# Recurrent stage of a hybrid decoder layer: one filler unit moved from the last head's end to the running sums, and a second accumulator bank for the first five units

## Chip, cores and metric

One Trainium2 chip, one NeuronCore. The metric is the device time of one execution in microseconds (us). Engine names in the rows: PE is TensorE (PEld its weight loads), DVE is VectorE, ACT is ScalarE, POOL is GpSimd, SP is SyncE.

## What is computed

One inference step of one decoder layer: 512 prompt tokens and 8 x 4 sample tokens (544 in all), model width 1024. The change touches the stage that computes the mLSTM branch. Cut to what matters here:

```python
# recurrent branch, per head h of 4 (DQK = 128, DV = 256)
b     = cumsum(log_f)                        # running sums over the tokens
m_t   = max(b + m, max_s(b_t - b_s + i_s))   # running maximum
s     = (q @ k.T) * exp(d_log - m_t)
num   = w_inter * (q @ C) + s @ v
C_new = a * C + (w * k).T @ v                # new state, also an output
y_a   = norm(num / max(|den|, exp(-m_t))) * norm_a_g * sigmoid(a_o)
# merge gates, needed two stages later
gates = sigmoid(x @ w_merge)                 # (544, 1024) @ (1024, 2048)
# next stage: learned block compressor of raw key/value pages
kc, vc = einsum(pages + pe, w_cmp)
```

## The kernel before

The program is a row of stages; between two stages all engines meet at a barrier. `stage_project` makes q, k, v and the gates' inputs, `stage_mlstm` (295 to 474 us of the profile) the recurrent branch, `stage_compress` (to 498 us) the block compressor, then attention, merging, a layer norm and the expert layer follow, which takes most of the time.

In `stage_mlstm` TensorE has two kinds of work. The recurrent products of the four heads depend on VectorE and ScalarE at many places. The **filler** is `x @ w_merge`, which depends on nothing of the stage: 16 weight tiles of 128 columns, each for two token halves of 256 and 288, make 32 **units**, numbered u = 0 to 31 (tile n = u // 2). A unit is 8 steps of 3 matmuls (high and low parts of both operands), 24 matmuls into one accumulator of PSUM. `fill(key)` issues the steps that the table `fill_at` gives to a place in the program: "scan" (before the running sums are used), "cols" (behind the small products that turn the sums into columns), and for each head the places "c", "e3" to "e0", "g", "u" and "end". Evens have 256 tokens, odds 288.

Around each unit other engines work in their own fixed order:

- ScalarE copies the finished accumulator to the staging tile `gate_stage` (`gates`, L1034; semaphore `g_evac`), and behind every odd unit of tile n it makes the high part of tile n + 2 (`high`, L1024).
- GpSimd makes the low part of that tile (`low`, L678); tile n's low part overwrites its raw weights.
- SyncE stores `gate_stage` (L652) once the odd unit's copy is made, and loads the weights of tile n + 3 (L641). All its transfers are issued in one fixed order. After the store of tile 15 come three loads for the next stage: `bqT` (L664, 2176 KB) and the two halves of the compressor's weights `wc` (L666, 1024 KB each), then four key/value pages `xs` (L671, 256 KB each), which wait until head 3's new state has been written out.

VectorE's part ahead of head 0 is a chain on four partitions: two ScalarE functions of the forget gate, two `tensor_tensor_scan` (L892, L894), then short operations up to `abr` (L906), which sets `m_ready`. TensorE waits for `m_ready` at L780, makes some 20 small products of 1 to 32 columns (L780 to L789), and goes on with the "cols" unit and head 0 (L798). Every head after that follows the same pattern; its last recurrent products are two groups at L847 that update the sample states, with the unit "u" between them and the unit "end" behind them. After head 3 TensorE turns two small results (L856, L857) and waits for the normalised rows (L870), which depend on a VectorE chain (L953 to L994), a square root on ScalarE (L1069) and 15 ScalarE scalings (L1075).

In `stage_compress` SyncE (L1137) and ScalarE (L1276) issue the last eight pages of 256 KB at the stage's start; TensorE's first series of 128 matmuls (`cmpX`, L1189) waits for `wc`, the second (`xs`, L1189) for all 16 pages.

Of the kernel before, what the change touches and what calls it, by code (L numbers as in the profile page):

```python
# [33 lines left out]
AH, DQK, DV = 4, 128, 256  # L34
# [505 lines left out]
def stage_mlstm(nc, s, io):  # L540
# [48 lines left out]
    gst = at("gate_stage", 8704, [P, 2, T])  # L589
    GT = 2 * DC  # L590
    fill_at, filled = {}, 0
    for key, steps in ([("scan", 24), ("cols", 8)] +
                       [((h, k), n) for h in range(AH)
                        for k, n in (("c", 16), ("e3", 8), ("e2", 4), ("e1", 4), ("e0", 4), ("g", 4), ("u", 8), ("end", 8))]):
        fill_at[key] = (filled, filled + steps)
        filled += steps
    assert filled == 16 * GT
# [2 lines left out]
    with ExitStack() as ctx:  # L600
# [18 lines left out]
        gwh_done, gwl_done, g_psum, g_evac, bq_in = (sem("gw_high"), sem("gw_low"), sem("gate_psum"), sem("gate_evac"),  # L619
                                                     sem("bq_in"))  # L620
        g_sent = [sem("g_sent0"), sem("g_sent1")]
        ps = ctx.enter_context(nc.psum_tensor("ps_m", [P, 8, 512], F32))
        block = ctx.enter_context(nc.Block())

        score_at = [(2, 0), (3, 0), (4, 0), (4, 256)]
        update_bank = [0, 5, 2, 3]

        def done_tiles(key):

            return range(fill_at[key][0] // 16, fill_at[key][1] // 16)  # L630
# [116 lines left out]
        def _(pe):  # L747
            def fill(key):

                for step in range(*fill_at[key]):  # L750
                    u, dc = step // 8, step % 8
                    n, half = u // 2, u % 2
                    t0, nt = TSPLIT[half]
                    out, toks = ps[:, 1, 0:nt], slice(t0, t0 + nt)
                    if dc == 0:
                        if n >= 2:
                            pe.wait_ge(gwl_done, n - 1)
                        if u:
                            pe.wait_ge(g_evac, u)
                    pe.matmul(out, gw_hi[:, n % 2, dc, :], s.xTh[:, dc, toks], start=(dc == 0), stop=False)  # L760
                    pe.matmul(out, gw_hi[:, n % 2, dc, :], s.xTl[:, dc, toks], start=False, stop=False)
                    last = pe.matmul(out, gw_lo[:, n % 3, dc, :], s.xTh[:, dc, toks], start=False, stop=(dc == DC - 1))
                    if dc == DC - 1:
                        last.then_inc(g_psum, 1)

            def slot(k):

                if k >= 2:
                    h, x = (k - 2) // 6, (k - 2) % 6
                    if 1 <= x <= 4:  # L770
                        pe.wait_ge(out_act, 4 * h + x)
                    else:
                        pe.wait_ge(out_dve, 2 * h + 1 + x // 5)
                return ps[:, 6 + k % 2, :]
# [18 lines left out]
            for h in range(AH):  # L793
# [24 lines left out]
                out = slot(6 * h)  # L818
# [6 lines left out]
                for k, j in enumerate((3, 2, 1, 0)):  # L825
# [3 lines left out]
                    out = slot(6 * h + 1 + k)  # L829
# [5 lines left out]
                out = slot(6 * h + 5)  # L835
# [185 lines left out]
        def _(act):  # L1021
# [4 lines left out]
            def gates(key):  # L1026

                for u in range(fill_at[key][0] // 8, fill_at[key][1] // 8):
                    n, half = u // 2, u % 2
                    t0, nt = TSPLIT[half]  # L1030
                    act.wait_ge(g_psum, u + 1)
                    if half == 0 and n >= 2:
                        act.wait_ge(g_sent[n % 2], 16 * (n // 2))
                    act.copy(gst[:, n % 2, t0:t0 + nt], ps[:, 1, 0:nt]).then_inc(g_evac, 1)  # L1034
                    if half == 1 and n + 2 < GT:
                        high(n + 2)

# [2247 lines left out]
```

## Time and profile before

| | us |
|---|---|
| median of 3 runs | 2167.01 (2165.47 to 2167.32) |
| profiled execution, its own time | 2169.9 |
| span of the profiled execution, first to last instruction | 2168.2 |
| mean granted TensorE clock in it | 0.988 of full speed |

Times in the rows are counted from the span's start. A row of a timeline that ends in [x <-E] says that the engine sat idle for x us before it and that an operation of engine E ended the wait. PEclk is the granted TensorE clock: 1.00 stands for 2.4 GHz, 0.50 for 1.2 GHz.

### The profile page before, as it was taken

What the parts mean: (1) busy time and instruction counts of PE and PEld (TensorE: products, weight loads), DVE (VectorE), ACT (ScalarE), POOL (GpSimd) and SP (SyncE); (2) the same over time, 40 slices, a digit from 0 to 9 for tenths busy, and PEclk for the clock granted to TensorE, in tenths of its full rate; (3) what the DMA queues carried; (4) which work ended last, traced back from release to release, by engine and by line L of the source; (5) the groups of instructions that cost most, each with busy time, mean ns of one, the idle gap of its engine ahead of it and who ended that gap; (6) DMA issues with size and microseconds to landing.
All of it is one profiled execution on the core that took longest, in us unless ns stands there. A gap on an engine that the chain in (4) does not pass through costs nothing.

```text
span 2168.2 us, 34384 instructions
## 1 busy us (share of the span) xinstructions
PE 2093.0 (97%) x13308; PEld 1861.3 (86%) x13308; DVE 1482.0 (68%) x3070; ACT 986.9 (46%) x1763; POOL 916.7 (42%) x615
## 2 busy tenths in 40 slices
PE   9999999978998998999999999999999999999998
PEld 8898988865655986999999999999998887888886
DVE  4334242456777455498889979876648899888886
ACT  2122322225777231333346666676544554445542
POOL 1000222331110001346877677777765555555530
PEclk9999999988999999999999999999999999999999
DMA  4354333456010533326889899999999999999992
GB/s 146 95 197 117 104 117 119 140 206 156 2 41 22 204 112 130 106 75 234 298 266 313 297 347 312 330 382 402 370 331 389 404 405 379 394 399 396 388 364 80
DMA packets 191242, 518.58 MB, mean 239 GB/s; under 512 B 15796, under 2 KB 85544, under 8 KB 186600
## 3 DMA queue, kind: packets, MB, share of 16 engines
q1 hardware_dynamic: 139656, 330.80, 43.4%
q0 software_dynamic: 50848, 184.53, 22.8%
q8 instruction: 106, 1.74, 0.3%
q10 hardware_dynamic: 576, 1.05, 0.1%
q14 instruction: 56, 0.46, 0.1%
HBM read 446.70 MB, written 73.75 MB: 240 GB/s over the span
## 4 chain that ended last, share of the span: by engine, by line
PE 56%; DVE 3%; ACT 0%; POOL 0%; issue 0%; DVEq 0%
PE ps_e L2559 24%; PE ps_e L2534 8%; PE ps_e L2529 7%; PE ps_e L2528 7%; PE ps_e L2551 3%; PE ps_e L2583 1%; PE ps_e L2589 1%; PE ps_e L2594 1%; PE ps_e L2590 1%; PE ps_e L2517 1%; DVE row L2924 1%; DVE one_b L2908 0%; DVE one_a L2908 0%; POOL u_lo L2477 0%; DVE oh L2842 0%
## 5 line engine op out<-in xcount | busy, mean ns | idle before, releaser
L2470 POOL DMA_INDIRECT row<-in_peer_v,sparse_idx x160 | 273.6, 1710 | 210.9 <-DVE y L2932 159.5
L2528 PE MATMUL ps_e<-hTh,u_hi 128*128 128x384 f32 x1024 | 347.1, 339 | 0.0
L2529 PE MATMUL ps_e<-hTl,u_hi 128*128 128x384 f32 x1024 | 346.7, 339 | 0.0
L2477 POOL TENSOR_TENSOR u_lo<-u_raw,u_hi 128x1024 fp32r<-128x1024 f32 x128 | 313.9, 2454 | 65.6 <-ACT u_hi L2634 56.9
L2559 PE MATMUL ps_e<-v_hi,w_hi 128*128 128x512 f32 x768 | 242.4, 397 | 0.0
L2559 PE MATMUL ps_e<-v_lo,w_hi 128*128 128x512 f32 x768 | 240.7, 394 | 0.0
L2559 PE MATMUL ps_e<-v_hi,w_lo 128*128 128x512 f32 x768 | 240.6, 394 | 0.0
L2952 DVE TENSOR_TENSOR v_lo<-v_raw,v_hi 128x1024 fp32r<-128x1024 f32 x128 | 158.1, 1237 | 85.0 <-ACT v_hi L2673 84.6
L2534 PE MATMUL ps_e<-hTh,u_lo 128*128 128x384 f32 x1024 | 207.7, 345 | 3.8 <-POOL u_lo L2477 3.8
L2673 ACT CAST v_hi<-v_raw 128x1024 fp32r<-128x1024 f32 x128 | 128.2, 1048 | 154.7 <-DMA v_raw<-in_peer_v 154.7
L2924 DVE CUSTOM_DVE_ANT_0 row<-row,ps_e 128x1024 f32<-128x1024 f32 x150 | 178.6, 1214 | 24.6 <-DMA row<-in_peer_u,sparse_idx 22.8
L2470 POOL DMA_INDIRECT row<-in_peer_u,sparse_idx x150 | 153.5, 1024 | 98.4 <-DVE sparse_hid L2924 75.7
L2528 PEld LDWEIGHTS ps_e<-hTh,u_hi 128*128 128x128 f32 x1024 | 193.0, 189 | 0.0
L2529 PEld LDWEIGHTS ps_e<-hTl,u_hi 128*128 128x128 f32 x1024 | 193.0, 189 | 0.0
L2534 PEld LDWEIGHTS ps_e<-hTh,u_lo 128*128 128x128 f32 x1024 | 176.4, 188 | 4.5 <-POOL u_lo L2477 4.5
L2559 PEld LDWEIGHTS ps_e<-v_hi,w_hi 128*128 128x128 f32 x768 | 145.1, 189 | 34.3 <-issue 0.8
L2559 PEld LDWEIGHTS ps_e<-v_lo,w_hi 128*128 128x128 f32 x768 | 144.6, 188 | 34.7
L2559 PEld LDWEIGHTS ps_e<-v_hi,w_lo 128*128 128x128 f32 x768 | 144.5, 188 | 33.8
L2932 DVE SCALAR_TENSOR_TENSOR y<-row,sparse_w,y 128x1024 f32<-128x1024 f32 x128 | 164.3, 1283 | 8.6 <-DMA row<-in_peer_v,sparse_idx 5.1
L250 PE MATMUL ps_proj<-xT_hi,w_hi 128*128 128x256 f32 (+2 forms) x528 | 151.8, 287 | 2.2 <-DVE xT_lo L332 1.7
L251 PE MATMUL ps_proj<-xT_lo,w_hi 128*128 128x256 f32 (+2 forms) x528 | 152.3, 289 | 0.0
L252 PE MATMUL ps_proj<-xT_hi,w_lo 128*128 128x256 f32 (+2 forms) x528 | 152.0, 288 | 0.0
(557 smaller groups left out, 4536.0 us busy)
## 6 DMA issues: line engine op xcount, KB each, us to landing
u_raw<-in_peer_uT SPq DMA_DIRECT2D x128, 512.0 KB
v_raw<-in_peer_v SPq DMA_DIRECT2D x30, 2048.0 KB, 10.4
hidden_gelu<-gelu_out SPq DMA_DIRECT2D x64, 384.0 KB
gate_tables<-g_buf SPq DMA_DIRECT2D x48, 512.0 KB
e_gate<-gate_tables SPq DMA_DIRECT2D x31, 768.0 KB
gelu_in<-hidden_gelu SPq DMA_DIRECT2D x31, 768.0 KB
w_raw<-in_w_tiles SPq DMA_DIRECT2D x45, 512.0 KB, 3.6
gw_raw<-in_merge_tiles SPq DMA_DIRECT2D x16, 512.0 KB, 3.9
```

Source lines behind the costliest of these rows:

```text
L250: pe.matmul(out, hi, s.xTh[:, dc, toks], start=(dc == 0), stop=False)
L251: pe.matmul(out, hi, s.xTl[:, dc, toks], start=False, stop=False)
L252: last = pe.matmul(out, lo, s.xTh[:, dc, toks], start=False, stop=(dc == DC - 1))
L2470: pool.indirect_dma_start(out=row[:, :], out_offset=None, in_=io.peer_u if i < U_END else io.peer_v, in_offset=bass.IndirectOffsetOnAxis(a ...
L2477: pool.tensor_tensor(u_lo[n % UB][:, :, :], u_raw[n % UB][:, :, :], u_hi[:, n % UH, :, :].bitcast(F32), ALU.subtract).then_inc(ul_done, 1)
L2528: pe.matmul(ps[:, n % 2, 0:TD], u_hi[:, n % UH, dc, :], hTh[:, dc, :], start=(dc == 0), stop=False)
L2529: pe.matmul(ps[:, n % 2, 0:TD], u_hi[:, n % UH, dc, :], hTl[:, dc, :], start=False, stop=False)
L2534: last = pe.matmul(ps[:, n % 2, 0:TD], u_lo[n % UB][:, dc, :], hTh[:, dc, :], start=False, stop=(dc == DC - 1))
L2559: last = pe.matmul(ps[:, 2 * t + half, :], w[u][:, c, ts], v[u][:, c, half * 512:(half + 1) * 512], start=(g == 0 and c == 0 and w is whi ...
L2924: dve.tensor_tensor_reduce(out=row, in0=row, in1=ps[:, 4:6, :], scale=1.0, scalar=0.0, op0=ALU.mult, op1=ALU.add, accum_out=hid[:, c:c + 1 ...
L2932: dve.scalar_tensor_tensor(out=acc, in0=row, scalar=wsp[:, c:c + 1], in1=acc, op0=ALU.mult, op1=ALU.add)\
L2952: dve.tensor_tensor(v_lo[g % 2][:, c, :], v_raw[g % 2][:, c, :], v_hi[g % 2][:, c, :].bitcast(F32), ALU.subtract).then_inc(vl_done, 1)
```

## The change

Three edits. The table gives the "scan" place 32 steps instead of 24 (units 0 to 3 instead of 0 to 2) and head 3's "end" none instead of 8; every place between thus works on the unit with the next number. The units 0, 2 and 4 accumulate in PSUM bank 7, all others in bank 1 as before. The wait ahead of a unit follows: unit 1 waits for no copy any more, units 2 to 5 for the copy of the unit before the last, later ones for the last as before.

```diff
-    for key, steps in ([("scan", 24), ("cols", 8)] +
+    for key, steps in ([("scan", 32), ("cols", 8)] +
                        [((h, k), n) for h in range(AH)
-                        for k, n in (("c", 16), ("e3", 8), ("e2", 4), ("e1", 4), ("e0", 4), ("g", 4), ("u", 8), ("end", 8))]):
+                        for k, n in (("c", 16), ("e3", 8), ("e2", 4), ("e1", 4), ("e0", 4), ("g", 4), ("u", 8),
+                                     ("end", 8 if h < AH - 1 else 0))]):
...
+        def fill_bank(u):
+
+            return 7 if u in (0, 2, 4) else 1
...
-                    out, toks = ps[:, 1, 0:nt], slice(t0, t0 + nt)
+                    out, toks = ps[:, fill_bank(u), 0:nt], slice(t0, t0 + nt)
                     if dc == 0:
                         if n >= 2:
                             pe.wait_ge(gwl_done, n - 1)
-                        if u:
+                        if u >= 6:
                             pe.wait_ge(g_evac, u)
+                        elif u >= 2:
+                            pe.wait_ge(g_evac, u - 1)
...
-                    act.copy(gst[:, n % 2, t0:t0 + nt], ps[:, 1, 0:nt]).then_inc(g_evac, 1)
+                    act.copy(gst[:, n % 2, t0:t0 + nt], ps[:, fill_bank(u), 0:nt]).then_inc(g_evac, 1)
```

**ScalarE, from the forget gate's logarithm (L1041) to the columns' exponentials (L1045).** The names in brackets are the semaphores waited for; a hardware semaphore used again shows the name of its first use, so x_in1, x_in7 and gw_in0 to gw_in2 are only labels. Before:

```order
L1041 ACTIVATE lfrow<-lfrow 4x544 [waits x_in1]
L1034 COPY gate_stage<-ps_m 128x256 [waits gate_psum]
L1034 COPY gate_stage<-ps_m 128x288 [waits gate_psum]
L1024 CAST gw_hi<-gw_raw 128x1024 [waits gw_in2]
L1034 COPY gate_stage<-ps_m 128x256 [waits gate_psum]
L1045 ACT_TABLE_LOAD
L1045 ACTIVATE en<-ps_m 128x16 [waits x_in7]
```

And in the changed program, whose lines are numbered 7 higher here:

```order
L1048 ACTIVATE lfrow<-lfrow 4x544 [waits x_in1]
L1041 COPY gate_stage<-ps_m 128x256 [waits gate_psum]
L1041 COPY gate_stage<-ps_m 128x288 [waits gate_psum]
L1031 CAST gw_hi<-gw_raw 128x1024 [waits gw_in2]
L1041 COPY gate_stage<-ps_m 128x256 [waits gate_psum]
L1041 COPY gate_stage<-ps_m 128x288 [waits gate_psum]
L1031 CAST gw_hi<-gw_raw 128x1024 [waits gw_in0]
L1052 ACT_TABLE_LOAD
L1052 ACTIVATE en<-ps_m 128x16 [waits x_in7]
```

The copy of unit 3 and the high part of tile 3, with its wait for that tile's load, now stand ahead of the columns' exponentials; before they stood behind them.

**GpSimd, from the marks of the sample states to the first operands of the state products.** Before:

```order
L710 TENSOR_TENSOR inside<-inside 128x2 [waits sample_marks]
L678 TENSOR_TENSOR gw_lo<-gw_raw,gw_hi 128x1024 [waits gw_high,sample_marks]
L715 DMA out_p_m<-brow 4x1 [waits x_in6]
L716 DMA out_s_m<-brow 4x8x1
L685 TENSOR_SCALAR kws<-kn,wsi 128x128
```

After:

```order
L715 TENSOR_TENSOR inside<-inside 128x2 [waits sample_marks]
L683 TENSOR_TENSOR gw_lo<-gw_raw,gw_hi 128x1024 [waits gw_high,sample_marks]
L683 TENSOR_TENSOR gw_lo<-gw_raw,gw_hi 128x1024 [waits gw_high]
L720 DMA out_p_m<-brow 4x1 [waits x_in6]
L721 DMA out_s_m<-brow 4x8x1
L690 TENSOR_SCALAR kws<-kn,wsi 128x128
```

The low part of tile 3 moved ahead of the two small stores and of the first head's operands.

**TensorE, from head 3's last full unit to the turned results.** Before:

```order
L762 MATMUL ps_m<-xT_hi,gw_lo 128x256
L847 MATMUL ps_m<-vn,kwb 128x257 [waits stage_out0]
L847 MATMUL ps_m<-vn,kwb 128x257 x3
L760 MATMUL ps_m<-xT_hi,gw_hi 128x288 [waits gate_evac,gw_low]
L761 MATMUL ps_m<-xT_lo,gw_hi 128x288
...
L856 MATMUL ps_m<-ident,nout 32x128 [waits stage_out0,proj_psum,stage_out1]
L857 MATMUL ps_m<-ident,pn 4x128
```

After:

```order
L769 MATMUL ps_m<-xT_hi,gw_lo 128x288
L854 MATMUL ps_m<-vn,kwb 128x257 [waits stage_out0]
L854 MATMUL ps_m<-vn,kwb 128x257 x3
L863 MATMUL ps_m<-ident,nout 32x128 [waits stage_out0,proj_psum,stage_out1]
L864 MATMUL ps_m<-ident,pn 4x128
```

The 24 matmuls of the "end" unit are gone from this place; unit 31 is now the one ahead of the second update group. SyncE's order is the same in both programs: only the events that it waits for come at other times.

## Rows read from the trace of the kernel before

**Rows 1.** Timeline of TensorE, running sums: start, length, engine, line, operation, [idle before it]

```profile
295.37 0.35 PE L760 MATMUL ps_m<-xT_hi,gw_hi 128*128 128x256 f32 x1 [2.10 <-PEq L78]
...
299.55 0.40 PE L760 MATMUL ps_m<-xT_hi,gw_hi 128*128 128x288 f32 x1 [1.10 <-ACT gate_stage L1034]
...
303.51 0.39 PE L760 MATMUL ps_m<-xT_hi,gw_hi 128*128 128x256 f32 x1 [0.49 <-ACT gate_stage L1034]
...
307.62 0.22 PE L780 MATMUL ps_m<-ident,brow 4*128 4x4 f32 x1 [0.99 <-DVE abr L906]
```

**Rows 2.** Timelines of ScalarE, GpSimd and VectorE, one after another, same stretch

```profile
303.35 1.05 ACT L1024 CAST gw_hi<-gw_raw 128x1024 fp32r<-128x1024 f32 x1
...
304.55 2.43 POOL L678 TENSOR_TENSOR gw_lo<-gw_raw,gw_hi 128x1024 fp32r<-128x1024 f32 x1 [6.46 <-ACT gw_hi L1024]
...
302.17 1.28 DVE L894 TENSOR_TENSOR_SCAN mrow<-lift_mask,arow 4x544 f32<-4x544 f32 x1
...
304.65 2.35 DVE L904 COPY rows<-mrow 4x32 f32<-4x32 f32 x1
...
307.41 0.15 DVE L906 TENSOR_TENSOR abr<-m,mrow 4x8 f32<-4x8 f32 x1
```

**Rows 3.** Sums over stretches: length, each engine's busy us, then PEclk, DMA share, GB/s

```profile
307.00:312.00 5.00, 4.38 (x30) 4.32 (x31) 0.67 (x8) 1.32 (x2) 0.00 (x0) 0.66 0.15 61
312.00:318.00 6.00, 6.00 (x29) 5.04 (x29) 0.41 (x4) 1.68 (x8) 2.64 (x5) 0.72 0.02 3
298.00:304.00 6.00, 4.41 (x32) 3.97 (x32) 4.47 (x6) 2.43 (x5) 0.09 (x1) 1.00 1.02 335
```

**Rows 4.** Timeline of TensorE at the end of head 3

```profile
456.57 0.50 PE L847 MATMUL ps_m<-vn,kwb 32*128 32x257 f32 x4
...
460.39 0.29 PE L762 MATMUL ps_m<-xT_hi,gw_lo 128*128 128x288 f32 x1
```

**Rows 5.** Timelines of VectorE, then ScalarE, behind head 3

```profile
461.67 0.24 DVE L989 TENSOR_SCALAR rstd<-den 128x16 f32<-128x16 f32 x2
...
461.14 1.28 ACT L1069 ACT_TABLE_LOAD   x1
...
463.64 0.60 ACT L1075 ACTIVATE hn<-vn,nbias,rstd 128x256 f32<-128x256 f32 x1 [0.90 <-DVE nbias L994]
```

**Rows 6.** Timeline of SyncE's DMA queue (SPq), end of this stage, start of the next

```profile
461.14 0.33 SPq L652 DMA_DIRECT2D gate_pre<-gate_stage  x1
461.52 1.26 SPq L664 DMA_DIRECT2D bqT<-bq_rows  x1
462.82 1.71 SPq L666 DMA_DIRECT2D wc<-in_w_cmp  x2
...
474.91 3.65 SPq L1137 DMA_DIRECT2D xs<-in_cache_cmp_T  x4
```

**Rows 7.** Sums over stretches around those transfers, columns as in rows 3

```profile
457.00:461.00 4.00, 3.90 (x34) 3.35 (x26) 3.46 (x15) 0.33 (x2) 0.93 (x1) 1.00 0.00 0
461.00:476.00 15.00, 6.10 (x40) 5.60 (x40) 10.91 (x34) 9.20 (x19) 2.79 (x24) 0.88 1.00 385
476.00:484.00 8.00, 6.18 (x128) 6.10 (x128) 7.36 (x26) 0.00 (x0) 7.58 (x12) 0.58 1.02 380
484.00:486.00 2.00, 0.41 (x8) 0.41 (x10) 1.43 (x8) 0.00 (x0) 0.57 (x1) 1.00 0.06 20
```

**Rows 8.** The view of tile xs, 440 to 500 us: issue to landing

```profile
DMA to landing us min/median/max: 2.9/6.0/11.5
```

**Rows 9.** Timeline of TensorE in the compression stage, and where attention begins

```profile
477.64 6.18 PE L1189 MATMUL ps_c<-cmpX,wc 128*64 128x33 f32 x128 [5.76 <-DMA wc<-in_w_cmp]
485.59 8.87 PE L1189 MATMUL ps_c<-xs,wc 128*64 128x128 f32 x128 [1.78 <-DMA xs<-in_cache_cmp_T]
...
498.58 0.49 PE L1414 MATMUL ps_a<-kslT,bqT 64*128 64x128 f32 x4 [1.86 <-PEq L78]
```

**Rows 10.** Sums over a stretch of TensorE's second series there

```profile
486.00:490.00 4.00, 4.00 (x48) 4.00 (x46) 0.00 (x0) 0.00 (x0) 0.00 (x0) 0.57 0.00 0
```

## Prediction

> **What bounds the kernel now.** I read the sums by stretch first, for the two places that the change touches, then the timeline of each engine there, and then followed the consequence through the transfers into the next stage. Most of the time is TensorE's work in the expert layer, which the change doesn't touch; what is won or lost between 295 and 498 us is carried through the stage barriers as it is. Three places count.
>
> *Running sums.* TensorE has nothing of its own until `m_ready` and works on units 0 to 2. It stops three times: 1.10 us ahead of unit 1 and 0.49 us ahead of unit 2, each time until ScalarE has emptied the one accumulator bank, and 0.99 us until VectorE has finished `abr` [rows 1]. VectorE is no faster because of GpSimd: the copy at 304.65 us takes 2.35 us for 32 columns and ends at 307.00, when GpSimd's low part ends (304.55 + 2.43 = 306.98) [rows 2].
>
> *Small products.* From 307.62 us on TensorE makes products of few columns, and the granted clock falls: a mean of 0.66 over 5 us and 0.72 over the next 6 us [rows 3]. At the low level, 1.2 GHz or 0.50, that is (1 - 0.66) / 0.5 x 5 = 3.4 us and (1 - 0.72) / 0.5 x 6 = 3.4 us, 6.8 us at half speed, or 3.4 us of lost work.
>
> *The last head.* The last unit's last matmul starts at 460.39 us [rows 4], but nobody on the recurrent path waits for it: VectorE's chain goes on to 461.67 + 0.24 = 461.91 us, and the scalings on ScalarE start at 463.64 us [rows 5]. What does wait for it is SyncE. The store of the last gate tile is issued at 461.14 us, and queued right behind it, in the fixed order, are `bqT` and `wc` [rows 6]. In the four microseconds before that the DMA engines carry nothing; then they are full, at 385 and 380 GB/s, until 484 us [rows 7]. That backlog is what TensorE waits for in the next stage: 5.76 us for `wc`, 1.78 us for the pages [rows 9].
>
> **Part by part.** *Two banks and a fourth unit in the running sums.* Units 1 and 2 take, to their modelled ends, 303.51 - 0.49 - 299.55 = 3.47 us and 307.62 - 0.99 - 303.51 = 3.12 us [rows 1]. Back to back each loses its tail and its restart, about 0.25 us together by the spacing of the matmuls, so a pair costs 6.1 us. Units 0 to 3 then run without a stop (unit 2 needs unit 0's copy, unit 3 needs unit 1's, both long made) from 295.37 to 307.6 us: the stops of 2.6 us and the tails pay for a whole unit.
>
> Is `m_ready` in time? Unit 1 ends about 1.4 us earlier, so the high part, at 303.35 us now, starts at 302.0, and the low part on GpSimd at 303.2 instead of 304.55 us. VectorE is then in the scan of 302.17 + 1.28 = 303.45 us [rows 2]. The rest of the chain stands behind GpSimd until 303.2 + 2.43 = 305.6 us, and needs the 1.9 us that it needs now without the stop (from 303.45 to 307.41 + 0.15 = 307.56, less 2.2): ready at 307.5. If GpSimd also has to wait for the scan, it ends at 303.45 + 2.43 = 305.9 and `m_ready` comes at 307.8. The small products start between 307.6 and 307.9 instead of 307.62 us: 0 to +0.3, I take +0.1, since a step of 0.3 needs a wait that no row shows. The Trainium skill ("SBUF — State Buffer", Who interferes with whom) says that the pair of ports that VectorE and GpSimd share is held for a whole instruction, also by a VectorE operation with two inputs in SBUF, and that the later one waits. By that rule GpSimd would wait for the scan, and the step would be the 0.3; it speaks against the change, but for little.
>
> *The copy of unit 3 and tile 3's high part on ScalarE* (1.5 us) now stand ahead of the columns' exponentials, and its low part ahead of `prepare` on GpSimd. TensorE's "cols" unit covers them: they end near 309.2 us, the columns' results come at 310 us or later, and `cols_read` is wanted only behind the unit, at 313 us. If tile 3's load is late this cover is gone (third rival).
>
> *Clock.* The idle time ahead of the small products goes; they themselves stay, some 2.5 us at full speed. Bounds: the fall stays as it is, 0, or the clock stays up, -3.4 us [rows 3]. The fall is not made by idle time alone: TensorE was busy for 4.38 of the 5 us [rows 3], and it falls again behind a pause of only 1.78 us and matmuls of 33 columns (0.57 of full clock over 486 to 490 us) [rows 9, 10]. So I expect the small products to bring it down in most executions, sometimes for one period instead of two: -0.8 us. The Trainium skill ("TensorE: Matmul & The Clock Gate", The HAM clock gate) calls the low level the idle one and has the clock follow how busy TensorE has been. Read as "busy is busy", the changed stretch, without idle time, would keep 2.4 GHz and the whole 3.4 us come back; the row of 4.38 busy us at 0.66 speaks against that reading.
>
> *The heads.* Between the small products and head 3's second update group lie 14 units of each size, before and after, so nothing changes there but the parity: each tile's high and low part fall one unit earlier in the program. Heads 0 and 2 take the pattern of 1 and 3, and the other way round. 0 us.
>
> *The missing "end" unit.* TensorE saves 4 us where it was not awaited: 0. ScalarE no longer copies unit 31 late, so its table load (461.14 + 1.28 = 462.42 us) is over before VectorE is ready at 461.91 us [rows 5]: the root, the scalings and the stage's end come 0.5 us earlier, with the +0.1 above 0.4.
>
> *Transfers.* Unit 31 now ends where unit 30 ended, just before 456.57 us [rows 4], 3.9 us (4.0 less the 0.1) ahead of now. With it go the store, `bqT` and `wc`, issued from 457.2 us on, into the empty DMA time. From 461 to 486 us pass 15 x 385 + 8 x 380 + 2 x 20 = 8.85 MB [rows 7]; eight pages of 256 KB, 2.1 MB, are those issued at the next stage's start. Of the other 6.75 MB some 1.35 MB (3.8 us at 350 GB/s) have gone before 461 us, so they are done at 461 + 5.4 / 0.385 = 475.0 us. `wc` lands about 3.5 us earlier, near 474 us, when the stage begins: the first series starts at once and is over before the pages are in. The pages are issued from 474.91 - 0.4 = 474.5 us on [rows 6]. A page alone takes 2.9 us to land [rows 8], 0.7 of it data, so new data flow from 476.7 us at the latest and last 2.1 / 0.38 = 5.5 us: 482.2 us instead of 484.2, -2.0 with a gap, and -3.5 if only the last issue counts (now at 474.91 + 3.65 - 0.34 = 478.2, then at 477.8, + 2.9 = 480.7 us). I take -2.6, nearer the first, since the bytes bind more than the issues. This contains the 0.4 us above, not adding to it. The second series starts near 483.0 instead of 485.59 us.
>
> **Sum.** -2.6 (pages) - 0.8 (clock) = -3.4 us, and attention begins at 495.2 instead of 498.58 us [rows 9]. The profiled execution took 2169.9 us, so 2166.5 in its terms; the runs' median is 2.9 us lower, which gives 2163.6 us.
>
> **Rivals.** 1. *The clock stays up* through the small products. For it: no idle time is left around them. Against: rows 3 and 10. Worth -2.6 - 3.4 = -6.0: 2161.0 us. Chance 0.18.
> 2. *The early transfers buy next to nothing.* The second series needs all pages, and the last are tied to the stage's start; if the pages still take their median 6.0 us [rows 8] from the issue, only the 0.4 us arrive, with the clock's 0.8 a gain of 1.2: 2165.8 us. For it: they still queue behind each other. Against: that median was measured behind a backlog that is now gone. Chance 0.20.
> 3. *Slower: tile 3's load is late.* It is issued some 2 us earlier than now, near 302.6 us, behind two state loads that keep the DMA engines full (1.02 from 298 to 304 us) [rows 3], and ScalarE now waits for it ahead of the exponentials. By its bytes it lands near 307 us, wanted at 308.1. It decides once it lands after some 311 us, for then `cols_read` misses 313 us; each microsecond beyond costs one, and from 315 us on the gain is gone. At 317 us: 2169 us. Chance 0.05.
> 4. *The forecast*: 0.57, with its own range of 2161.8 to 2165.6, which takes in the pages' bounds and one clock period more or less (1.7 us) in the second series, where the pause ahead may grow from 1.78 to 3 us.
>
> **Numbers.** 0.2% of 2167 is 4.3 us, about what a measurement of this kernel can tell from no change. Faster by more than that: rival 1 and a quarter of the forecast's case, 0.33. Slower by more: 0.04. Within it: 0.63. The range that leaves two in ten out reaches from rival 1's upper half to rival 2: 2160.2 to 2166.6 us.
>
> **What would show it.** In the changed kernel's profile: no stop of TensorE between 295.4 and 307.6 us; GpSimd's low part at 303.2 to 303.5 and a VectorE operation of over 2 us behind it; the clock over 307 to 318 us (0.66 and 0.72 now); the store, `bqT` and `wc` near 457.2 us with transfers from there on; TensorE's first series at about 474 without a wait for `wc`, its second near 483 us. The forecast is wrong if the second series starts after 485, if head 0 begins later than 316.8 us, or if the later stages don't keep the distance.

## The result, and the profile after

The changed kernel takes 2172.3 us (median of 14 runs, 2167.92 to 2178.08), the kernel before 2168.16 us on the same chips (14 runs, 2165.47 to 2172.84; the three runs shown ahead of the prediction had a median of 2167.01). The ratio is 1.0022, 95% interval 1.0015 to 1.0029: slower by 4 to 5 us, where 3.4 us faster was forecast. The profiled execution took 2173.22 us, with a span of 2171.5 us.

The running sums went as intended. The timeline of TensorE there, then those of VectorE, GpSimd and ScalarE, to be held against [rows 1, 2]:

```profile
295.10 0.55 PE L767 MATMUL ps_m<-xT_hi,gw_hi 128*128 128x256 f32 x1 [2.09 <-PEq L78]
...
299.52 0.29 PE L767 MATMUL ps_m<-xT_hi,gw_hi 128*128 128x288 f32 x1
...
308.83 0.22 PE L787 MATMUL ps_m<-ident,brow 4*128 4x4 f32 x1
...
301.90 1.28 DVE L901 TENSOR_TENSOR_SCAN mrow<-lift_mask,arow 4x544 f32<-4x544 f32 x1
304.48 2.38 DVE L912 TENSOR_TENSOR rows<-m,mrow 4x32 f32<-4x32 f32 x1
307.16 0.16 DVE L913 TENSOR_TENSOR abr<-m,mrow 4x8 f32<-4x8 f32 x1
...
304.40 2.41 POOL L683 TENSOR_TENSOR gw_lo<-gw_raw,gw_hi 128x1024 fp32r<-128x1024 f32 x1 [6.58 <-ACT gw_hi L1031]
...
309.60 1.04 ACT L1031 CAST gw_hi<-gw_raw 128x1024 fp32r<-128x1024 f32 x1 [0.26 <-DMA gw_raw<-in_merge_tiles]
```

No matmul of the four units has an idle time behind it any more, and the small products follow unit 3 at once. Unit 0 alone ran at half clock in this execution, but for its last matmuls (it takes 299.52 - 295.10 = 4.42 us; with full clock it takes 2.93 us, as in experiments 1 and 12), which is why they start at 308.83 and not at 307.6 us. The sums over stretches, with columns as in [rows 3]:

```profile
295.00:298.50 3.50, 3.40 (x16) 3.43 (x17) 1.28 (x2) 3.40 (x4) 2.40 (x9) 0.51 0.09 14
307.00:312.00 5.00, 5.00 (x48) 4.79 (x47) 0.68 (x8) 2.73 (x3) 1.28 (x1) 1.00 0.68 190
312.00:318.00 6.00, 6.00 (x29) 4.83 (x28) 0.69 (x3) 0.93 (x7) 3.67 (x6) 0.72 0.19 71
```

The clock is up over 307 to 312 us (0.66 before), though until 308.83 us that stretch still holds matmuls of unit 3. TensorE is at the low clock for 3.4 us here, where it was for 6.8 us before, and that gives back what unit 0 lost: the second update group of head 3 starts at 456.21 us, where [rows 4] has 456.57. Up to here the change is level or 0.4 us ahead. What follows is the timeline of SyncE's queue, and then GpSimd's issue of head 3's state store, against [rows 6]:

```profile
456.74 0.33 SPq L657 DMA_DIRECT2D gate_pre<-gate_stage  x1
457.11 0.43 SPq L669 DMA_DIRECT2D bqT<-bq_rows  x1
457.59 0.94 SPq L671 DMA_DIRECT2D wc<-in_w_cmp  x2
473.58 3.65 SPq L676 DMA_DIRECT2D xs<-in_cache_cmp_T  x4
479.18 3.65 SPq L1144 DMA_DIRECT2D xs<-in_cache_cmp_T  x4
...
459.16 0.91 POOL L739 DMA_DIRECT2D out_s_C<-c  x1 [19.63 <-DVE nout L964]
```

The kernel before has, for the store and then for GpSimd's first operation in the next stage:

```profile
459.52 0.93 POOL L734 DMA_DIRECT2D out_s_C<-c  x1 [14.20 <-DVE nout L957]
...
474.20 0.20 POOL L1142 TENSOR_SCALAR_AFFINE_SELECT hm<-ones 128x16 f32<-128x16 f32 x1 [8.08 <-POOLq L78]
```

The view of waits over 440 to 500 us has this line for SyncE's queue in the changed kernel (us in total, times, longest):

```profile
SPq L674 <- DMA out_s_C<-c: 14.3, 1, 14.3
```

`bqT` is issued 4.4 us earlier, where 3.9 were forecast. But SyncE then waits 14.3 us for the landing of `out_s_C`, the state store of head 3, because it may load pages 4 to 7 only once that state has been written out (`c_sent[1]`); the kernel before has there:

```profile
SPq L669 <- DMA out_s_C<-c: 0.2, 1, 0.2
```

The store is issued 0.36 us earlier than before and takes 13.7 us to land. Why it does is seen in the DMA queues over windows (packets, MB, share of 16 engines); q1 carries SyncE's transfers, q0 GpSimd's. The changed kernel over 459 to 462, 462 to 465 and 465 to 468 us:

```profile
q1 hardware_dynamic: 58, 1.01, 94.1%
...
q1 hardware_dynamic: 51, 0.89, 84.6%
q0 software_dynamic: 17, 0.07, 5.6%
...
q1 hardware_dynamic: 109, 0.80, 64.4%
q0 software_dynamic: 107, 0.44, 35.4%
```

and the kernel before over the first two of them:

```profile
q0 software_dynamic: 82, 0.34, 30.3%
...
q0 software_dynamic: 190, 0.71, 67.2%
q1 hardware_dynamic: 111, 0.24, 32.8%
```

Before, the store has the DMA engines to itself from 461 to 464 us; the packets of q1 in the second window are those of the gate store (0.24 MB / 111, 2 KB each), and `bqT` comes behind them. Now the engines are full of `bqT` when the store is issued; its first packet comes behind 464 us, some 5 us after the issue (one-microsecond windows show none before), and from there on the two queues get the same number of packets, 107 and 109. A packet of the store is 4 KB (0.44 MB / 107), one of `bqT` 17 KB (0.89 MB / 51), one of `wc` 8 KB (0.27 MB / 33 over 468 to 469 us), so an equal number of packets is a third of the bytes or less for the store.

TensorE in the next stage, then GpSimd's first operation there, against [rows 9]:

```profile
478.65 5.79 PE L1196 MATMUL ps_c<-cmpX,wc 128*64 128x33 f32 x128 [7.59 <-PEq L78]
487.99 9.65 PE L1196 MATMUL ps_c<-xs,wc 128*64 128x128 f32 x128 [3.56 <-DMA xs<-in_cache_cmp_T]
...
501.75 0.49 PE L1421 MATMUL ps_a<-kslT,bqT 64*128 64x128 f32 x4 [1.86 <-PEq L78]
...
478.47 0.20 POOL L1149 TENSOR_SCALAR_AFFINE_SELECT hm<-ones 128x16 f32<-128x16 f32 x1 [13.22 <-POOLq L78]
```

SyncE's four page issues end at 473.58 + 3.65 = 477.2 us, and the stage's barrier opens only then: GpSimd begins at 478.47 us, where the kernel before has 474.20. TensorE waits for the barrier and no longer for `wc`. The last eight pages go out 479.18 - 474.91 = 4.3 us later, the second series starts 2.4 us later, runs 0.8 us longer at a lower clock, and attention begins 501.75 - 498.58 = 3.2 us later. The span is 3.3 us longer: the rest of the kernel adds nothing.

### The profile page after: what moved, and what is told of

Its sections match the earlier page's. It is cut to its first block, busy times and chain, and to the rows that moved or that the text cites. A ratio compares the mean times of both kernels' runs of the same rounds, so it can differ in the third digit from the quotient of the medians.

```text
span 2171.5 us, 34384 instructions
## 1 busy us (share of the span) xinstructions
PE 2093.4 (96%) x13308; PEld 1862.3 (86%) x13308; DVE 1485.0 (68%) x3070; ACT 987.6 (45%) x1763; POOL 920.5 (42%) x615
## 4 chain that ended last, share of the span: by engine, by line
PE 56%; DVE 3%; ACT 0%; POOL 0%; issue 0%; DVEq 0%
PE ps_e L2566 24%; PE ps_e L2541 8%; PE ps_e L2536 7%; PE ps_e L2535 7%; PE ps_e L2558 3%; PE ps_e L2590 1%; PE ps_e L2596 1%; PE ps_e L2601 1%; PE ps_e L2597 1%; PE ps_e L2524 1%; DVE row L2931 1%; DVE one_b L2915 0%; DVE one_a L2915 0%; POOL u_lo L2484 0%; DVE oh L2856 0%
## 6 DMA issues: line engine op xcount, KB each, us to landing
gelu_in<-hidden_gelu SPq DMA_DIRECT2D x31, 768.0 KB, 13.2
```

## The experiments

Theory S, formed from these rows: the moved unit does what it was meant to do, and the loads that it releases early overtake the state store, whose landing holds SyncE, the pages and the barrier. Its rival U: the unit, the second bank or the clock costs the time, and the store is a by-product. Each experiment's time is a median of 5 to 12 runs; the kernel before ran beside them, at 2168.80 (first four experiments), 2168.10 (next four), 2168.95 (next three) and 2168.82 us (last).

**1. The store ahead of the loads**, in the changed kernel, by SyncE instead of GpSimd:

```
+            sp.wait_ge(c_new, AH)
+            sp.dma_start(io.s_C[:, AH - 1]..., c0[:, (AH - 1) % 2, :, 0:DV]).then_inc(c_last, 16)
             sp.dma_start(s.bqT[:, :, :], io.bq_rows).then_inc(bq_in, 16)
...
-            sp.wait_ge(c_sent[1], 32)
+            sp.wait_ge(c_last, 16)
```

> The changed kernel, but head 3's new state is written out by SyncE, ahead of bqT and wc in its own queue, instead of by GpSimd. Theory S (in the changed kernel this store stands behind bqT and wc in the DMA engines, lands at 473 us instead of about 465, and holds up the four pages and the stage's end): the store lands near 464 us, the four pages are issued near 464 to 468 us, the compression stage begins near 473.5 us and its second series near 483 to 484 us; the time is 1 to 3.5 us below the kernel before. Rival U (the moved unit or the bank itself costs the time, in the sums, the heads or the clock): the second series may come earlier, but the time stays 3 to 5 us above the kernel before.

2167.31 us, ratio to the kernel before 0.9996 (0.9988 to 1.0005). The store lands 5.3 us after its issue at 458.99 us, SyncE waits 1.9 us for it, and attention begins at 495.66 us. The 4 us are gone, as S expected, with the moved unit and both banks in place; whether it is faster than the kernel before, which S also expected (by 1 to 3.5 us), this run does not show, since its interval holds 1.

**2. The banks alone**: the last filler unit stays at head 3's end, the banks alternate.

```
-    for key, steps in ([("scan", 32), ("cols", 8)] +
+    for key, steps in ([("scan", 24), ("cols", 8)] +
...
-                                     ("end", 8 if h < AH - 1 else 0))]):
+                                     ("end", 8))]):
```

> The two banks alone; the table of units is that of the kernel before. Theory S: unit 31 and the loads behind it stay where they were, TensorE only waits longer for the running sums (until about 307.6 us), so the time is within 1 us of before. Rival U: running the first units back to back costs 2 us or more by itself, by a later end of the running sums or a lower clock.

2168.09 us, ratio 1.0001 (0.9992 to 1.001), no difference. The gate store goes out at 459.87 us, behind the state store's issue, and SyncE waits 0.2 us for the latter.

**3. The move alone**, made in the kernel before, with its one bank:

```
-    for key, steps in ([("scan", 24), ("cols", 8)] +
+    for key, steps in ([("scan", 32), ("cols", 8)] +
...
-                        for k, n in (..., ("u", 8), ("end", 8))]):
+                        for k, n in (..., ("u", 8), ("end", 8 if h < AH - 1 else 0))]):
```

> The moved unit alone, with one bank. The three stops of the running sums stay, so unit 3 ends near 310.5 us, and everything behind it is 2.5 to 3 us later than in the changed kernel. Theory S: unit 31 still ends ahead of head 3's new state, the store still queues behind bqT and wc (over 10 us to landing), and the time is 6 to 8 us above before. Rival U, if the bank is what costs: the time is nearer to before than the changed kernel's, under +4 us.

2174.2 us, ratio 1.0027 (1.0017 to 1.0038). SyncE waits 13.7 us for the store, the barrier comes at 479.4, attention at 503.80 us. The move alone brings the loss; the direction and the wait are as S expected, the size (5.4 us of medians) is a little under its 6 to 8. About 1 us of it is not the store's: with one bank the four units stop three times, and the second update group of head 3 starts at 457.60 us instead of 456.57.

**4. The kernel before with a late store**: nothing is moved, but GpSimd issues head 3's store only once the last gate tile has landed.

```
                 pool.wait_ge(c_new, h + 1)
+                if h == AH - 1:
+                    pool.wait_ge(g_sent[1], 16 * DC)
```

> The kernel before, but GpSimd holds head 3's state store until the last gate tile has landed, which is when bqT and wc are already queued. No unit is moved. Theory S: the store takes 10 us or more, the four pages are issued at 474 us or later, the compression stage begins at 479 us or later, and the time is 5 us or more above before. Rival U: no unit was moved, so the time is within 1 us of before.

2177.98 us, ratio 1.0042 (1.0029 to 1.0055). GpSimd issues the store at 463.32 us, behind `bqT` and `wc`. SyncE's wait, and then the timeline of TensorE with the next stage's two series:

```profile
SPq L669 <- DMA out_s_C<-c: 15.4, 1, 15.4
```

```profile
483.62 6.84 PE L1191 MATMUL ps_c<-cmpX,wc 128*64 128x33 f32 x128 [12.15 <-PEq L78]
494.37 10.10 PE L1191 MATMUL ps_c<-xs,wc 128*64 128x128 f32 x128 [3.91 <-DMA xs<-in_cache_cmp_T]
```

The same kind of wait, and a barrier 9.2 us later than in the kernel before (GpSimd begins at 483.44 us), with no unit moved: the order of store and loads is enough by itself. The store's later issue, by 3.8 us, would not have been by itself: had it landed after 5.3 us as in experiment 1, the pages would have been issued by some 472.3 us (an estimate, 463.32 + 5.3 + 3.65), ahead of the old barrier at 474.20. Instead the pages go out at 478.56 us.

**5. Small rows**: in the changed kernel `bqT` comes in eight transfers with rows of 2 KB.

```
-            sp.dma_start(s.bqT[:, :, :], io.bq_rows).then_inc(bq_in, 16)
+            for q in range(BH // 2):
+                sp.dma_start(s.bqT[:, q, :], io.bq_rows[:, q, :]).then_inc(bq_in, 16)
...
-            sp.wait_ge(bq_in, 16)
+            sp.wait_ge(bq_in, 16 * (BH // 2))
```

> The changed kernel, with bqT (2176 KB) loaded by eight transfers whose rows are 2176 bytes instead of one whose rows are 17 KB. Theory S (the head-3 state store comes late because its packets of 4 KB take turns, one for one, with packets of 17 KB and 8 KB, and the page loads behind it hold the stage barrier): beside bqT the store now gets some two thirds of the bytes instead of a fifth, and lands 6 to 9 us after its issue instead of 13.7; the last four pages are issued at 466 to 469 instead of 473.6 us, the barrier no longer waits for SyncE, and the kernel gives back most of the loss: 0 to 1.5 us above the kernel before. Rival Q (what counts is only how many bytes were handed to the engines ahead of the store, not the size of their packets): the eight issues still come before 460.5 us, the store still takes over 11 us, pages at 471 us or later, and the kernel stays 3 to 5 us above the kernel before.

2169.68 us, ratio 1.0006 (0.9997 to 1.0015). The store lands 9.8 us after its issue instead of 13.7, the pages go out at 468.68 us, the barrier no longer waits for SyncE, attention begins at 494.66 us. The queues of this kernel over 464 to 467 us:

```profile
q0 software_dynamic: 207, 0.82, 66.5%
q1 hardware_dynamic: 214, 0.43, 36.8%
```

Again an equal number of packets, but now they are two thirds of the bytes for the store. Rival Q, bytes ahead and nothing else, falls by these counts, not by the landing time: 9.8 us lies between S's 6 to 9 and Q's 11 or more, and eight issues take SyncE so long that `wc` goes out at 459.99 us, behind the store's issue at 458.13, so there were also fewer bytes ahead. The first packet of the store still comes some 4 us or more after its issue (one packet in the window from 462 us, 49 in the next). The median, 1.6 us above the kernel before, doesn't show the attention's early start: the profiled execution took 2165.57 us, but seven of the eleven runs took 2169.6 us or more, and why is open.

**6. The kernel before with SyncE's store** (the edit of experiment 1).

> The kernel before, with head 3's state store issued by SyncE ahead of bqT, as in the run of the changed kernel with that edit. It tells what the moved unit is worth once the store comes first. Theory S: in the kernel before the store came first anyway, so only little changes, within 1.5 us of the kernel before; the last gate tile still ends at 461.1 us, bqT is issued near 461.9 us, the attention begins at 497.5 to 499 us, some 2 to 3 us later in the profile than in the changed kernel with the same edit (495.66). Rival W (the gain of that run came from the store's queue and not from the earlier transfers): the attention begins here at 496.5 us or earlier, and the time is the same as that of the changed kernel with the edit.

2169.77 us, ratio 1.0009 (1.0 to 1.0018), 1.7 us above the kernel before and so just outside S's 1.5; `bqT` issued at 461.77 us, attention at 499.22 us. SyncE can issue the store only behind the last gate store, at 461.30 us, 1.8 us later than GpSimd did. Rival W falls: the gain of experiment 1 isn't the store's queue.

**7. The changed kernel with SyncE's store again**, on the same chip as 6.

> The changed kernel with SyncE's store ahead of bqT, once more, on the chip of the other three, to be set against the kernel before with the same edit. Theory S with the forecast's gain left over: attention begins at 495.5 to 496.5 us, and the time is 0 to 3 us under the kernel before and 1 to 3 us under the kernel before with this edit. Rival: the 2.9 us at the attention's start are not carried to the end, and both kernels with SyncE's store take the same time within 1 us.

2167.08 us, ratio 0.9994 (0.9985 to 1.0003), attention at 494.93 us. With SyncE's store in both kernels, the whole change (moved unit and banks) is worth 2169.77 - 2167.08 = 2.7 us of medians: all eleven runs here took under 2168.3 us, ten of the eleven of experiment 6 over 2168.5. Attention comes 4.3 us earlier in the profiled executions, 1.3 us of it because the second series ran at full clock here (7.21 us) and not there (8.54). Part of the 2.7 us is what SyncE's late store costs experiment 6: against the unchanged kernel before, this one is 1.0 us faster, within the interval. And what the moved unit adds to the banks no run shows: on one chip, experiments 1 and 2 differ by 0.8 us, far less than their runs scatter.

**8. The loads level with the store**: one more wait in the changed kernel, on the state.

```
+            sp.wait_ge(c_new, AH)
             sp.dma_start(s.bqT[:, :, :], io.bq_rows).then_inc(bq_in, 16)
```

> The changed kernel with one more wait: SyncE issues bqT and wc only once head 3's new state is ready (459.0 us by the run with SyncE's store), 2.2 us later than in the changed kernel and about with the store on GpSimd's queue. Nothing else moves. Theory S gives a dose between: the store has a head start or an even start, lands 6 to 11 us after its issue (13.7 in the changed kernel), the last four pages are issued at 466 to 471 us, and the time is -1 to -4 us against the changed kernel. Rival U (the moved unit itself, or the clock at the stage's start, costs the 4 us): the same time as the changed kernel or later, 2172 us or more.

2174.03 us, ratio 1.003 (1.0018 to 1.0041): by its time alone, what U expected. This expectation of S was wrong, and the trace shows why. SyncE and GpSimd issue:

```profile
457.22 0.32 SPq L670 DMA_DIRECT2D bqT<-bq_rows  x1
...
457.49 0.91 POOL L740 DMA_DIRECT2D out_s_C<-c  x1 [19.63 <-DVE nout L965]
```

Over 460 to 462 us, and then over 463 to 464 us, the engines carry this:

```profile
q1 hardware_dynamic: 46, 0.80, 96.2%
...
q1 hardware_dynamic: 16, 0.28, 75.1%
q0 software_dynamic: 18, 0.07, 17.8%
```

Not one packet of the store in 4.5 us, then one for one with `bqT`, a fifth of the bytes, and it lands after 14.6 us. An issue at the same moment is no even start: GpSimd's store needs 1.5 us or more to its first packet on free engines, and three times that on full ones. So the head start had to be larger, and the two theories were still to be parted by it. One part of U falls here: unit 0 ran at full clock (1.00 over 295 to 298.5 us), and the time was lost all the same.

**9. The loads 2.4 us behind the store**: the same wait, on VectorE's sums under the roots.

```
+            sp.wait_ge(var_ready, 2)
             sp.dma_start(s.bqT[:, :, :], io.bq_rows).then_inc(bq_in, 16)
```

> The changed kernel, with SyncE holding bqT and wc until VectorE has the sums under the square roots ready (some 461.4 us, 2.3 us behind the state store's issue; in the kernel before the distance is 2.0 us). The run that held them only until the state was ready kept them level with the store, and the store's first packet still came 5 us after its issue. Theory S (the transfers' order at the engines): with the head start of before, the store's first packets come within 2 us of its issue and it lands 5 to 7 us after it, the pages are issued near 465.5 us, SyncE no longer holds the barrier, and the time is within 1.5 us of the kernel before, 3 to 5 us below the changed kernel. Rival U (the moved unit, the second bank or the clock costs the 4 us): the same time as the changed kernel, 3 us or more above the kernel before.

2166.6 us, ratio 0.9994 (0.9985 to 1.0003). SyncE, GpSimd's issue, then TensorE:

```profile
459.42 0.32 SPq L670 DMA_DIRECT2D bqT<-bq_rows  x1
459.79 1.69 SPq L672 DMA_DIRECT2D wc<-in_w_cmp  x2
463.10 3.65 SPq L677 DMA_DIRECT2D xs<-in_cache_cmp_T  x4
471.60 3.65 SPq L1145 DMA_DIRECT2D xs<-in_cache_cmp_T  x4
...
457.04 0.91 POOL L740 DMA_DIRECT2D out_s_C<-c  x1 [19.63 <-DVE nout L965]
...
474.78 6.20 PE L1197 MATMUL ps_c<-cmpX,wc 128*64 128x33 f32 x128 [5.90 <-DMA wc<-in_w_cmp]
482.69 8.87 PE L1197 MATMUL ps_c<-xs,wc 128*64 128x128 f32 x128 [1.71 <-DMA xs<-in_cache_cmp_T]
...
495.67 0.49 PE L1422 MATMUL ps_a<-kslT,bqT 64*128 64x128 f32 x4 [1.86 <-PEq L78]
```

and its queue over 459 to 461 us:

```profile
q0 software_dynamic: 171, 0.70, 98.0%
```

The store lands in 5.3 us, and with all parts of the change in place the kernel is 5.6 us faster than the changed kernel (2172.18 us, below). A wait added, and nothing else: rival U is out. Another rival for the late first packet, that VectorE's work holds up GpSimd's store, falls too: VectorE is busy for 3.26 of the 4 us from 457 us here and for 3.28 in experiment 8, in the same chain of operations, and only here do packets come within 2 us of the issue.

**10. The loads behind the store's landing**: the wait is on `c_sent[1]`, and SyncE issues `bqT` at 466.03 us.

> The changed kernel, with SyncE holding bqT and wc until the state store has landed, near 464.8 us. The other end of the dose: the store is undisturbed, the pages are issued right behind, and nothing of the forecast's early transfers is left: bqT and wc come 3.3 us later than in the kernel before. Theory S: the store lands 5 to 6 us after its issue, wc some 2 to 3 us later than in the kernel before, the second series starts near 487 to 488 us, and the time is 1 to 3 us above the kernel before, still below the changed kernel by 1 to 3 us. Rival U: as its 4 us stay and the late loads come on top, 6 us or more above the kernel before.

2169.48 us, ratio 1.0001 (0.9992 to 1.001). The store lands in 5.0 us, `wc` is waited for 7.40 us, the second series starts at 488.22 and attention at 499.54 us. As late as that the loads cost what the change gains, and the kernel is still 2.7 us under the changed one. Against the kernel before it is 0.5 us slower, where S expected 1 to 3.

**11. The changed kernel once more**, beside 9 and 10.

> The changed kernel once more, beside the two kernels with held loads and on their chip: 3.5 to 5.5 us above the kernel before, store landing 13 to 15 us after its issue, attention beginning near 501.5 us. Both theories expect the same of it; it is the level against which the other two are read.

2172.18 us, ratio 1.0017 (1.0008 to 1.0026), 3.2 us above the kernel before, a little less than expected; the store takes 13.2 us, attention begins at 501.72 us.

**12. Experiment 9 once more**, on another chip.

> The changed kernel with bqT and wc held until the sums under the square roots are ready, once more, to see whether it is under the kernel before or only level with it. Theory S with the forecast's gain left over: 1 to 3.5 us under the kernel before (2.35 us of medians in the first run), attention beginning between 495.5 and 498 us. Rival: the first run's distance was its chip's, and this one is level with the kernel before within 0.7 us.

2166.69 us, ratio 0.9995 (0.9985 to 1.0004), attention at 494.20 us, earlier than the 495.5 expected. Both times the median is some 2 us under that of the kernel before (2.35 and 2.13), and both intervals hold 1: that this version is faster than the kernel before is likely, not shown; that it is faster than the changed kernel is shown.

**The traces from a common start.** The profiled executions reach unit 0 at different times, from 294.79 to 296.97 us, so up to 2.2 us between two of the times above is made ahead of this stage. Here they are counted from the start of unit 0; the barrier is GpSimd's first operation of the next stage. The last column is the median less that of the kernel before beside it.

| kernel | unit 0 starts | barrier | second series | attention | median |
|---|---|---|---|---|---|
| before | 295.37 | 178.8 | 190.2 | 203.2 | |
| changed | 295.10 | 183.4 | 192.9 | 206.7 | +4.1 |
| changed once more (11) | 294.93 | 182.9 | 193.0 | 206.8 | +3.2 |
| move alone (3) | 295.18 | 184.0 | 194.9 | 208.6 | +5.4 |
| before, late store (4) | 295.12 | 188.3 | 199.3 | 213.5 | +9.2 |
| loads level (8) | 294.92 | 182.8 | 193.7 | 207.9 | +5.9 |
| before, SyncE's store (6) | 295.15 | 179.3 | 191.4 | 204.1 | +1.7 |
| loads behind the landing (10) | 296.97 | 179.3 | 191.3 | 202.6 | +0.5 |
| small rows (5) | 295.56 | 178.3 | 187.8 | 199.1 | +1.6 |
| banks alone (2) | 296.48 | 177.3 | 188.2 | 199.5 | -0.7 |
| SyncE's store (1) | 296.70 | 176.4 | 187.6 | 199.0 | -1.5 |
| SyncE's store again (7) | 296.24 | 176.4 | 187.4 | 198.7 | -1.0 |
| loads 2.4 us behind (9) | 296.00 | 174.9 | 186.7 | 199.7 | -2.4 |
| the same again (12) | 294.79 | 176.5 | 188.1 | 199.4 | -2.1 |

The five rows in which the store goes out level with the loads or behind them, with their large packets, have the barrier at 182.8 us or later, and all others at 179.3 or earlier: theory S holds on this count as well. But the traces set the better kernels some 4 us ahead of the kernel before, where the medians say 1 to 2.4, or nothing for the banks alone. In part this is the clock of one execution: the second series took 7.21 us in experiments 1, 2, 5, 7, 10 and 12, and 8.54 to 8.87 us in experiments 6 and 9 and in the kernel before.

## Why the prediction was wrong, and where it was right

*Running sums* (units back to back, small products +0.1): right. There is no stop, and the four units take 13.7 us instead of the forecast's 12.2, of which 1.5 is unit 0 at half clock. In experiments 1, 5, 7, 8, 9 and 12, with unit 0 at full clock, they take 12.2 us. The half clock doesn't need the change: the kernel of experiment 4, with nothing moved, has 0.57 over 295 to 298.5 us, and that of experiment 9, with all of it, 1.00. But both traces of the changed kernel itself have 0.51, so that it is chance is not shown. GpSimd's low part was to be at 303.2 to 303.5 us; it came at 304.40, by unit 0's delay, and the operation of VectorE that started right behind it took 2.38 us for 32 columns, as in [rows 2]. The Trainium skill ("SBUF — State Buffer", Who interferes with whom) has it that of two operations that need the shared ports the later one waits for the whole of the first. The trace agrees here, with GpSimd's operation ending at 306.81 and VectorE's at 306.86 us. The other collision that it was cited for, with the scan, could not be seen: the scan was over at 303.2 us.

*Tile 3's high part*: covered, as forecast. Its load held ScalarE for 0.26 us only; the slower rival named there played no part.

*Clock*: under-sized. Forecast were 0.8 us; over 307 to 312 us the granted clock went from 0.66 to 1.00, (1.00 - 0.66) x 5 = 1.7 us at 2.4 GHz, and over 312 to 318 us it stayed at 0.72. Weighed over the 11 us, nine of the ten executions with 32 steps have 0.85, the banks alone 0.84, and the three with neither 0.69, so half of the low stretch goes nearly always, not sometimes. The tenth, that of experiment 9, has 1.00: there the forecast's first rival came true. Stops ahead of the small products don't decide this by themselves, as the move alone has three of them (1.10, 0.49 and 0.46 us) and 0.85 too. The gain didn't reach the end in the changed kernel, as unit 0 used it up.

*The heads* and *the missing unit* at head 3's end: right. The second update group moved by -0.36 us and the scalings on ScalarE from 463.64 to 462.78 us.

*Transfers* (-2.6 us): this step failed. It said that the store of the last gate tile, `bqT` and `wc` go "into the empty DMA time", and worked out from bytes alone when they are through, and it took the stage's end and the pages' issue at 474.5 us as free of them. The time was empty because the state store of head 3 had not been issued yet; it is issued at 459.5 us, in the middle of the 3.9 us by which the loads were to come forward, and SyncE's next instruction waits for it. The step counted what moves with the gate store and passed over what it moves past: the store's 1 MB is in its 6.75 MB, but with no place in the order and nobody who waits for it. In place of 474.5 us the pages went out at 479.18 us, +4.3 instead of -0.4, and the 2.6 us of gain became 2.4 us of loss, with 0.8 us more from the lower clock of the second series. That series began at 487.99 us, past the 485 us that the forecast had named as the sign of being wrong. The rival that ended on the slower side named another load in another place; this mechanism was not among the cases.

Where the order is kept, the forecast's total nearly comes out: in experiments 1, 7, 9 and 12 attention begins 3.5 to 4.5 us earlier than before, counted from unit 0, where it has 3.4, and the medians give 1.0 to 2.4. That the traces come near is in part luck, since the parts are others. In experiments 1, 7 and 12 the second update group comes 1.6 us earlier (159.6 us from unit 0 instead of 161.2), which is the clock, twice its 0.8. The second series starts 2.1 to 2.9 us earlier, so the transfers add 0.5 to 1.3 us, not 2.6. The rest, 8.87 - 7.21 = 1.7 us, is the clock of the second series, which the forecast had in its range only. The sum of bytes is not tested by this: with the order safe no run had the loads go out more than some 3.4 us earlier (experiments 1 and 7), and what the full head start would be worth stays open.

That packets decide how the two queues share, and not bytes, could have been read beforehand. The Trainium skill ("DMA: Bandwidth & Descriptors", Queues, rings and completion order) says that a DMA engine takes turns between the queues that have work for it, one packet each. The trace agrees, with 107 packets against 109 here, 207 against 214 in experiment 5 and 18 against 16 in experiment 8. With the packet sizes of the traces this makes a third of the bytes for the store beside `wc` and a fifth beside `bqT` (0.07 of 0.35 MB in experiment 8).

What stays open: what sets unit 0's clock; and why the store's first packet comes 5 us after its issue on full engines, which taking turns doesn't explain by itself. It goes the other way too: in the kernel before, SyncE's last gate store is issued at 461.14 us, while GpSimd's store fills the engines, has one packet ahead of 464 us, and takes 4.7 us to land, where it takes 2.1 us in the changed kernel:

```profile
gate_pre<-gate_stage SPq DMA_DIRECT2D x1, 272.0 KB, 4.7
...
gate_pre<-gate_stage SPq DMA_DIRECT2D x1, 272.0 KB, 2.1
```

## What to carry to other kernels

When a transfer comes forward, list every transfer that it passes on every queue, with its packet size and with who waits for its landing: idle DMA time just ahead of a backlog may be the only time in which a small, awaited store gets through. Earlier is not always sooner: here loads 2.4 us behind the store were best, loads level with it or ahead of it cost some 6 to 8 us more, and one added wait turned the loss into a kernel at least level with the one before. Run each part of a change alone: here the move alone had the whole loss, and the banks alone had no difference in time. And count the times of two traces from a common start, since one profiled execution can differ from the next by 2 us before it reaches the place in question.

## What was not expected of the hardware

- Two queues with work share the engines by packets: 107 to 109 with packets of 4 and 8 KB, 207 to 214 with 4 and 2 KB, 18 to 16 with 4 and 17 KB.
- A store by GpSimd's queue sends its first packet 1.5 to 2 us after the issue when the engines are free (459.52 us, first packets in the window from 461), and 4 to 6 us after it when they are full (459.16 us, first in the window from 464; 457.49 us, window from 462). A 1 MB store lands after 5.0 to 5.3 us in the one case and 13.2 to 14.6 us in the other. A store of 272 KB by SyncE's queue, issued behind GpSimd's, landed after 4.7 us instead of 2.1.
- Products of a few columns behind four units of large matmuls kept 2.4 GHz for 3.2 us in the changed kernel (from 308.83 us, granted clock 1.00 until 312 us), and for some 3.7 us in experiment 3, with stops between the units (from 310.27 us, 1.00 until 314 us). Behind three units with stops it was 1.2 us in the kernel before (from 307.62 us, 0.78 over 308 to 309 us).
- The first 3.5 us of the stage, behind a pause of 2.1 us, ran at a granted clock of 0.51 in both executions of the changed kernel and at 1.00 in others with the same filler units (experiments 1 and 9), 1.5 us of difference.
